# Turning the next head's queries and keys one 512-token fill a step (steps 3, 5, 6, 7) instead of two fills in steps 5 and 6, in both attentions of a one-layer trunk

## The reference, cut to what matters

```python
def causal_block_attention(q, k, v, log_forget_cum=None):
    for i in range(seq // Q_BLOCK):                 # Q_BLOCK = 128, seq = 1024
        q_lo, q_hi = i * Q_BLOCK, (i + 1) * Q_BLOCK
        qb, kb, vb = q[:, q_lo:q_hi], k[:, :q_hi], v[:, :q_hi]
        s = jnp.einsum('bqhd,bkhd->bhqk', qb, kb).astype(jnp.float32) * scale
        if log_forget_cum is not None: s = s + (c_q - c_k)
        mask = (q_lo + jnp.arange(Q_BLOCK))[:, None] >= jnp.arange(q_hi)[None, :]
        p = jax.nn.softmax(jnp.where(mask, s, NEG_INF), axis=-1).astype(v.dtype)
        outs.append(jnp.einsum('bhqk,bkhd->bqhd', p, vb))

def mixer_block(h, ...):
    proj = h @ w_in                      # latents, fox q/k/v, forget logits, u, gate logits
    o_mla = causal_block_attention(q_mla, k_mla, v_mla)            # 4 heads, q and k 96 wide, v 64
    o_fox = causal_block_attention(q_fox, k_fox, v_fox, cum_log_f) # 4 heads, q and k 64 wide, v 64
    o_s5 = s5_branch(u, ...)
    gates = jax.nn.sigmoid(gate_logits)
    merged = sum over the three branches of gates * (branch @ w_branch)
    return merged @ w_out                # then a gated feed-forward layer with a short convolution
```

## Time and profile before

| what | value |
|---|---|
| median of 3 runs | 1647.36 us (1645.93 to 1648.49) |
| the profiled execution's own time | 1651.23 us |
| its span | 1649.4 us |
| PE busy | 1521.9 us, 92% |
| PE weight loads busy | 1265.8 us, 77% |
| DVE busy | 939.9 us, 57% |
| ACT busy | 621.7 us, 38% |
| POOL busy | 126.6 us, 8% |
| mean granted TensorE clock | 0.967 |

### The profile page before, as it was taken

One profiled execution on the slowest core, in us unless ns is written; L12 is line 12 of the kernel. 1 busy time (PEld: TensorE's weight loads), 2 busy tenths in 40 slices (PEclk: granted clock), 3 DMA queues, 4 the chain that ended last, 5 costly groups with the idle time before them and its releaser, 6 DMA issues. The chain is left out here.

```text
span 1649.4 us, 19066 instructions
## 1 busy us (share of the span) xinstructions
PE 1521.9 (92%) x7214; PEld 1265.8 (77%) x7214; DVE 939.9 (57%) x1290; ACT 621.7 (38%) x1013; POOL 126.6 (8%) x104
## 2 busy tenths in 40 slices
PE   5999999987997988787899978999999999999999
PEld 4899877776576777676678767888888888888887
DVE  4310345666285665674783557887778887433333
ACT  4310224541222554212452335555555555332322
POOL 1000150002033000310120100000000000000000
PEclk9899999997998999898999989999999999999999
DMA  5130131103022000313455112322222221644643
GB/s 193 44 121 1 47 94 34 38 27 130 19 83 66 31 26 26 90 48 113 156 190 215 54 39 64 102 77 90 77 77 90 90 77 68 212 148 145 245 143 138
DMA packets 126500, 153.65 MB, mean 93 GB/s; under 512 B 11530, under 2 KB 94397, under 8 KB 126141
## 3 DMA queue, kind: packets, MB, share of 16 engines
q1 hardware_dynamic: 126224, 152.40, 28.3%
q10 hardware_dynamic: 189, 0.08, 0.0%
HBM read 115.55 MB, written 36.31 MB: 92 GB/s over the span
## 5 line engine op out<-in xcount | busy, mean ns | idle before, releaser
L486 PE MATMUL ps<-split_arena 128*128 128x512 f32 x1152 | 298.9, 414 | 25.3 <-ACT plain_arena L521 8.6
L1715 PE MATMUL ps<-split_arena 128*128 128x512 f32 x1320 | 308.0, 390 | 4.7 <-DVE split_arena L2253 3.5
L1715 PEld LDWEIGHTS ps<-split_arena 128*128 128x128 f32 x1320 | 247.8, 188 | 57.2 <-DVE split_arena L2253 4.0
L486 PEld LDWEIGHTS ps<-split_arena 128*128 128x128 f32 x1152 | 221.9, 198 | 74.1 <-issue 21.3
L1805 PE MATMUL ps<-down_w,down_a 128*128 128x512 f32 x352 | 137.3, 390 | 0.7 <-DVE down_w L1782 0.7
L1807 PE MATMUL ps<-down_w,down_a 128*128 128x512 f32 x352 | 137.1, 390 | 0.0
L1806 PE MATMUL ps<-down_w,down_a 128*128 128x512 f32 x352 | 137.1, 390 | 0.0
L1778 DVE TENSOR_TENSOR down_a<-plain_arena,down_a 128x1024 fp32r<-128x1024 f32 x44 | 53.9, 1225 | 144.5 <-ACT down_a L1767 144.5
L1715 PE MATMUL ps<-up_b,split_arena 128*128 128x512 f32 x528 | 130.7, 398 | 5.0 <-DVE split_arena L1643 4.9
L1715 PEld LDWEIGHTS ps<-up_b,split_arena 128*128 128x128 f32 x528 | 101.7, 193 | 27.1 <-DVE split_arena L1643 5.2
L1767 ACT ACTIVATE down_a<-plain_arena 128x1024 fp32r<-128x1024 f32 x44 | 46.7, 1061 | 161.6 <-PE ps L1807 146.5
(11 more groups left out here) (333 smaller groups left out, 2495.5 us busy)
## 6 DMA issues: line engine op xcount, KB each, us to landing
plain_arena<-scr_act SPq DMA_DIRECT2D x44, 512.0 KB, 3.6
plain_arena<-in_w_in SPq DMA_DIRECT2D x24, 512.0 KB, 4.2
scr_gate<-plain_arena SPq DMA_DIRECT2D x48, 256.0 KB, 2.0
plain_arena<-scr_gate SPq DMA_DIRECT2D x24, 512.0 KB, 4.6
plain_arena<-in_w_up SPq DMA_DIRECT2D x22, 512.0 KB, 5.1
up_raw<-in_w_up SPq DMA_DIRECT2D x22, 512.0 KB, 5.1
scr_act<-plain_arena SPq DMA_DIRECT2D x22, 512.0 KB, 2.6
plain_arena<-in_w_down SPq DMA_DIRECT2D x44, 256.0 KB, 3.9
```

The costliest lines, as they stand in the source:

```text
L486: mm = nc.tensor.matmul(m.ps[:, self.banks[half], :], w[:, k, :], src[:, k, h * BANK:(h + 1) * BANK], start=(j == 0), stop=(j == self.PER_ ...
L1715: mm = nc.tensor.matmul(o, self.w[j][w][:, k, :], self.h[j][k][h], start=(j in self.OPENS and k == 0 and n == 0), stop=(k == self.HK - 1 a ...
```

## The change

The transposes of the next head's queries and keys, their high and their low parts, stood in pairs: q0 and q1 in step 5, k0 and k1 in step 6. They now stand one in a step: q0 in step 3, q1 in step 5, k0 in step 6, k1 in step 7, on PE, ACT and DVE alike, in the three heads of each attention that have a next one. Their place inside a step is the same as before. Two waits go with it: ACT's high part of q0 waits for the first 4 scores of the head instead of all 8, and a score waits for the half of the keys that it reads (the first for blocks 0 to 3, the second for 4 to 7) instead of both. The number of instructions is the same.

```diff
--- before.py
+++ after.py
@@ -572,12 +573,20 @@
 
         fills = [(w, 0, half) for w in "qk" for half in range(2)]
         for s in range(ATT_STEPS):
-            h, i = divmod(s, TT)
-            if h + 1 < H and i in (5, 6):
-                fills += [("qk"[i - 5], h + 1, half) for half in range(2)]
-            fills += [("p", s, a, min(4, i + 1 - a)) for a in range(0, i + 1, 4)]
+            fills += self.turned_in(s)
+            fills += [("p", s, a, min(4, s % TT + 1 - a)) for a in range(0, s % TT + 1, 4)]
         self.fills = fills
         self.upto = {f[:2]: n + 1 for n, f in enumerate(fills)}
+        self.at = {f: n for n, f in enumerate(fills)}
+
+    def turned_in(self, s):
+
+        h, i = divmod(s, TT)
+        which = {3: ("q", h + 1, 0), 5: ("q", h + 1, 1), 6: ("k", h + 1, 0), 7: ("k", h + 1, 1)}
+        return [which[i]] if i in which and h + 1 < H else []
+
+    def qk_fills(self, s):
+        return [self.at[x] for x in self.turned_in(s)]
 
     def fills_of(self, what, n):
         return [f for f, x in enumerate(self.fills) if x[:2] == (what, n)]
@@ -602,7 +611,7 @@
     def score(self, pe, s):
         nc, m, kd = self.m.nc, self.m, self.kd
         h, i = divmod(s, TT)
-        pe.wait_ge(self.lo, self.upto["k", h])
+        pe.wait_ge(self.lo, self.at["k", h, i // 4] + 1)
         if s >= 2:
             pe.wait_ge(self.exped, s - 1)
         keys = (i + 1) * P
@@ -650,15 +659,13 @@
         self.score(pe, 0)
         self.score(pe, 1)
         for s in range(ATT_STEPS):
-            h, i = divmod(s, TT)
-            last = h + 1 == H
-            if i == 7 and not last:
+            i = s % TT
+            if i == 7 and s + 1 < ATT_STEPS:
                 self.score(pe, s + 1)
             if s + 2 < ATT_STEPS and i != 6:
                 self.score(pe, s + 2)
-            if not last and i in (5, 6):
-                for f in self.fills_of("qk"[i - 5], h + 1):
-                    self.turn(pe, f)
+            for f in self.qk_fills(s):
+                self.turn(pe, f)
             pe.wait_ge(self.normed, s + 1)
             for f in self.fills_of("p", s):
                 self.turn(pe, f)
@@ -689,7 +696,8 @@
             if n >= 0:
                 act.wait_ge(self.pv, n + 1)
         elif x[1]:
-            act.wait_ge(self.scores, TT * x[1])
+
+            act.wait_ge(self.scores, TT * (x[1] - 1) + (4 if x[0] == "q" and x[2] == 0 else TT))
         (hi, _), src = self.place(f)
         self.m.nc.scalar.activation(hi, src, ACT.Copy).then_inc(self.hi, 1)
 
@@ -730,16 +738,15 @@
                 self.split_hi(act, f)
         self.exponent(act, 0)
         for s in range(ATT_STEPS):
-            h, i = divmod(s, TT)
+            i = s % TT
             if s + 1 < ATT_STEPS:
                 self.exponent(act, s + 1)
             if s % 4 == 1 and s > 4:
                 self.out_low(act, s // 4 - 1)
             if s % 4 == 2 and s > 4:
                 self.out_hi(act, s // 4 - 1)
-            if h + 1 < H and i in (5, 6):
-                for f in self.fills_of("qk"[i - 5], h + 1):
-                    self.split_hi(act, f)
+            for f in self.qk_fills(s):
+                self.split_hi(act, f)
             for f in self.fills_of("p", s):
                 self.split_hi(act, f)
             self.fill.scalar(act, ATT_FILL[i])
@@ -799,8 +806,8 @@
                     self.split_lo(dve, f)
             if s + 2 < ATT_STEPS and i != 6:
                 self.maximum(dve, s + 2)
-            if not last and i in (5, 6):
-                for f in self.fills_of("qk"[i - 5], h + 1):
+            if s < ATT_STEPS:
+                for f in self.qk_fills(s):
                     self.split_lo(dve, f)
             if s % 4 == 1 and s > 4:
                 self.out_sum(dve, s // 4 - 1)
```

## The result

The change makes the kernel slower by 0.24%: the ratio to the kernel before is 1.0024, with a 95% interval of 1.0014 to 1.0034. The medians are 1651.01 us (1649.24 to 1655.95, 15 runs) against 1647.62 us (1644.87 to 1650.37, 15 runs). By the ratio the loss is 3.95 us; the prediction was 4.4.

The account below looks back on a forecast made before the run. PE was taken to bound the kernel, so only its idle time counted. Six transitions at 0.8 us (+4.8) less 0.4 at the start gave 1647.36 + 4.4 = 1651.8 us; own range 1649.5 to 1654.5, 8-in-10 range 1646.0 to 1656.0.

Parts of the forecast that it names:

- Step 3, q0 alone: Four transposes added in step 3 cost PE 0.42 us; DVE's idle 0.91 us covers the extra low part.
- Step 5, q1 alone: In step 5 the wait moves from p5a to p5b and stays; gate matmuls start 0.17 us earlier.
- Step 6, k0 alone: In step 6 p6b, not p6a, waits for k0's low part; PE is then 0.77 us ahead.
- Step 7, k1 added: In step 7 0.59 us waits before k1, a new wait of about 1 us before p7b; gate matmuls 0.8 us later.
- Step 8 and after: ACT's copy of gate bank 7 and the next nine gate matmuls move 0.8 us too; loss neither grows nor returns.
- Rival 4: In step 8 ACT's copy comes one piece (0.6 us) later, delaying the next nine gate matmuls; +8.0 us, 1655.4 us, chance 0.10.
- The start: First scores wait for half the keys: gain 0.4 us in fox (bounds 0 and 0.6), 0 in mla.
- The signs of being wrong: Wait before p7b under 0.3 us, waits in steps 5 or 6 halved, or granted clock in the attentions leaving 0.97.
- The sum: Whole kernel: +4.8 us over six transitions less 0.4 at the start, +4.4 us, giving 1651.8 us.

Follow-up runs that it names:

- e1: The change with k1 turned back in step 6 behind k0 instead of in step 7; ratio 0.9988 to the kernel before.
- e3: The change with k1 turned one step later, in step 0 of its own head; ratio 0.9958 to the kernel before.
- e8: The change with DVE making the low parts of p6 ahead of the maximum in step 7; ratio 0.9980 to the kernel before.
- e10: The kernel before with only DVE's low parts of p6 put ahead of the maximum in step 7; ratio 0.9964.
- e2: The kernel before with the relaxed wait alone: a score waits for the half of the keys it reads, turns stay in pairs; ratio 0.9983.
- e5: The change, but in head 0 of each attention every score waits for both halves of the keys; ratio 1.0020 to the kernel before.
- e4: The change with q0 turned in step 3, k0 in 5, q1 and k1 in steps 0 and 1 of their own head; ratio 0.9946 to before.
- e6: The change again, unaltered, run beside e5 on the same chip; ratio 1.0026 to the kernel before.
- e7: As e4, with head 0 treated alike: only q0 and k0 turned ahead of the first score; ratio 0.9935 to the kernel before.
- e9: e7 with DVE's low parts of p6 ahead of the maximum in step 7; 1633.93 us, ratio 0.9903 to the kernel before.

## Why the prediction was right, step by step

**Step 3, q0 alone.** Predicted 0.42 us of PE and nothing behind it. The four transposes take 254.16 - 253.73 = 0.43 us, and neither the turn of p3 nor the next step waits.

**Step 5, q1 alone.** Predicted: the wait goes from p5a to p5b and the gate matmuls start 0.17 us earlier. It is there, 1.04 us before the last two transposes, and e1, where this is all that is left in the transitions, gains 0.13 to 0.16. I gave the maximum as what stands in front. The DVE timeline after shows that this was only half the reason:

```profile
262.46 1.23 DVE L763 TENSOR_REDUCE stat<-ps 128x1 f32<-128x1024 f32 x1 [2.35 <-PE ps L624]
263.61 0.67 DVE L776 TENSOR_TENSOR split_arena<-ps,split_arena 66x512 fp32r<-66x512 f32 x1
```

```profile
262.90 0.59 ACT L702 ACTIVATE split_arena<-ps 66x512 fp32r<-66x512 f32 x1 [1.36 <-PE ps L608]
```

The high part of q1, on ACT, ends at 263.49 and the maximum at 263.69 (DVE starts the next instruction 0.08 us before the end shown). Without the maximum the low part could start 0.1 us earlier and no more: the road and the maximum are equally long here. That was read from the trace and not tried.

**Step 6, k0 alone.** Predicted 0.60 us gained against the step before (0.77 in all). From the gate matmuls of step 5 to those of step 6 it was 4.72 us before and is 268.66 - 264.53 = 4.13: 0.59.

**Step 7, k1 added.** Predicted a wait of about 0.6 us before k1 and one of about 1 us before p7b, and a transition 0.8 us longer. They are 0.50 and 0.85 (in the profile's idle time, which leaves out some 0.15 us by which instructions otherwise overlap), and the transition is 0.79 longer, in four of six; the two others are those with a stretch at half clock. From the start of k1's turn to the end of its low part it is 273.87 + 0.69 - 272.58 = 1.98 us, where the prediction took 1.97 from k0. Nearly all of that is work on this one fill: four transposes 0.63, its high part 0.59, its low part 0.69, with 0.03 to 0.04 us between them. e1 (k1 away), e3 (k1 where it is covered) and e8 (the first link cut) each took out the part that this reading gives them, within 0.15 us.

**Step 8 and after.** Predicted: the loss neither grows nor is given back. ACT's copy started at 276.00 and the nine gate matmuls at 276.74, 1.72 us behind the three of step 7, as before (278.02 - 276.30). Rival 4 did not come.

**The start.** Predicted 0.4 us in fox, 0 in mla. From the second pair of turns to the scores of step 2 it took 242.69 - 238.46 = 4.23 us in fox before and 241.86 - 238.24 = 3.62 after: 0.6, the upper bound, as the DMA that holds ACT's copy had landed earlier in this execution (the copy started at 239.99 without a wait; before, at 241.14 behind 0.82 us for the DMA). In mla the table load held the exponent as foreseen:

```profile
520.75 1.28 ACT L712 ACT_TABLE_LOAD   x1
522.04 0.37 ACT L712 ACTIVATE plain_arena<-ps,stat 128x128 f32<-128x128 f32 x1
```

It went from 522.13 to 522.04, and the turns before it by 0.08 (518.46 to 518.38): no gain.

**The signs of being wrong.** Two of the three that the prediction names did not come: the waits of steps 5 and 6 stayed, and the one before p7b was 0.85 us. The third did, by a little: the granted clock of both windows of the earlier trace rows, 0.97 before, is 0.98 after (profile columns as there).

```profile
235.00:382.00 147.00, 127.50 (x767) 105.31 (x765) 85.54 (x173) 70.57 (x153) 9.59 (x4) 0.98 0.12 35
514.00:661.00 147.00, 128.86 (x772) 106.90 (x770) 85.81 (x173) 70.56 (x152) 9.58 (x4) 0.98 0.11 34
```

**The sum.** 6 x 0.79 - 0.6 = 4.1 us by the profiles, 4.4 predicted, 3.95 by the ratio (2.3 to 5.6). The clock is not in the sum, and the prediction took it as unchanged: its mean nearly was (0.967 before, 0.970 after), but the half-clock stretches fell elsewhere, and each of them in a transition was worth 1.1 to 1.6 us (27.74 - 26.67, 28.24 - 26.67). In this pair both attentions together, each from its first turn of q to the last gate matmuls of step 7, were only some 1.5 us longer after, not 4.1; the rest was given back at half-clock stretches that went. So the agreement of the sum to 0.5 us is partly luck: the part that the runs confirm closely is the 0.79 us a transition. The three executions of the change's order bear one in mla each; that would add some 1.6 us, within the interval. The prediction's own range was also added up a little too narrow: from the bounds that it names (3.6 and 6.0, 0 to 0.6 off, 1.4 around them) it is 1649.0 to 1654.8 us, not 1649.5 to 1654.5. The measured time lies in both.

**The rule of the Trainium skill.** "Perfetto Trace Analysis", Optimization Strategy, says that a repeated gap can mean too little SBUF or PSUM, and bids to make the dependency start sooner or complete faster. The first half agrees with these runs: the gap is a wait for one of two banks. The second half does not say which start to move: splitting the fills over the steps gave +0.79 us a transition, while an earlier low part where DVE was idle, which is that rule too, gave -0.77 (e10). A later turn where matmuls cover it helped as well (e3: -0.43).

## What to carry to other kernels

Where work goes round several engines and back (here PE, ACT, DVE, PE, 2.0 us), taking one fill out of a pair hardly shortens the wait: what is waited for is the road of the first fill alone, and what stands in front of it. A smaller fill would have a shorter road; that was not tried. Count how many such roads end in a wait, and put each where independent work of its length follows before its result is asked for; spreading them evenly may add a road that nothing covers. And before moving a transfer, look whether an idle engine sits behind an instruction that waits: swapping two independent instructions on DVE was worth 0.77 us a transition, as much as the change had cost.

## What the runs showed of the hardware that I had not expected

Stretches at half clock wander between executions of nearly the same program. At the start of mla the granted clock over 6.8 us was 0.50 before and 1.00 after, though PE had waited 1.4 and 0.8 us there. In mla's head 1 a stretch of about 3.4 us at half clock followed the same waits of steps 5 and 6 in all three executions of the change's order and in neither e3 nor e8, which have these waits too. I could not tie them to one wait. With the relaxed wait mla's first nine gate matmuls took 2.3 us in four of seven profiled kernels with four fills ahead of the first score (the change, e2, e3, e8), with the old wait in none of three (before, e5, e10: 3.89 to 4.19 us). That points to the start without showing it.

What the transitions leave open lies in such stretches in good part. Every execution has a mean granted clock on record. Over the 75 executions of the kernel before that were taken beside e1 to e10, 0.001 more of it goes with 0.8 us less (correlation -0.64). And every kernel of the experiments has more of it than the kernel before beside it. The last column is what the ratio gives beyond the waits: beyond the transitions at full clock and, where the wait is relaxed, 0.6 us for the start.

| kernel | mean clock, this and before beside it | worth at 0.8 us per 0.001 (an estimate) | gain left over by the waits |
|---|---|---|---|
| e1 | 0.9702, 0.9693 | 0.7 us | 0.6 us |
| e2 | 0.9722, 0.9693 | 2.3 us | 2.2 us |
| e3 | 0.9728, 0.9693 | 2.8 us | 3.7 us |
| e4 | 0.9710, 0.9693 | 1.4 us | 2.6 us |
| e5 | 0.9705, 0.9682 | 1.8 us | 1.4 us |
| e6 | 0.9693, 0.9682 | 0.9 us | -0.2 us |
| e7 | 0.9720, 0.9682 | 3.0 us | 4.4 us |
| e8 | 0.9715, 0.9689 | 2.0 us | 3.2 us |
| e9 | 0.9730, 0.9689 | 3.2 us | 5.0 us |
| e10 | 0.9714, 0.9689 | 2.0 us | 1.2 us |

Each difference of two mean clocks is uncertain by about 0.001, so each estimate by some 0.8 us, and the ratios by 1.5 us and more. Why these orders have fewer stretches at half clock, and whether all of the rest is the clock, stays open. Such stretches make one profiled execution worth little for a difference of 0.2%, while the transitions at full clock repeat within 0.04 us from kernel to kernel.
